# Two chained transformer blocks on one core: logits taken from the unscaled rows, and the gather of the expert tokens as two products of rounded parts

## The reference

```
h = h + mix
u = rmsnorm(h, norm_ffn_w)                      # h / rms(h) * w
g_logits = u @ router_group_w + b               # 4 groups
e_logits = (u @ router_expert_w + b)[group]     # 8 experts in a group
top 2 experts of the best group, weights g_prob * softmax(top 2)
y[token] = sum of weight * (silu(u @ gate[e]) * (u @ up[e])) @ down[e]
out = rmsnorm(h + y, norm_final_w)
```

## Time and profile before

| | |
|---|---|
| median, lowest, highest of 3 runs | 1380.79, 1374.78, 1382.4 us |
| the profiled execution's own time | 1377.91 us |
| its span, first to last instruction | 1376.1 us |
| busy share PE, DVE, ACT, POOL | 94%, 44%, 34%, 4% |
| mean granted clock of PE | 0.978 |
| DMA traffic | 349.86 MB |

### The profile page before, as it was taken

One profiled execution on the slowest core, in us unless ns is written; L12 is line 12 of the kernel. 1 busy time (PEld: TensorE's weight loads), 2 busy tenths in 40 slices (PEclk: granted clock), 3 DMA queues, 4 the chain that ended last, 5 costly groups with the idle time before them and its releaser, 6 DMA issues. The chain is left out here.

```text
span 1376.1 us, 18603 instructions
## 1 busy us (share of the span) xinstructions
PE 1290.4 (94%) x8067; PEld 958.5 (70%) x8067; DVE 605.0 (44%) x925; ACT 470.5 (34%) x688; POOL 60.9 (4%) x57
## 2 busy tenths in 40 slices
PE   6898869999999999799999999889999999999996
PEld 3886758999998989679999999644344443434432
DVE  2776667344556586485755556431110111101112
ACT  3643545433444644444554454211000000000001
POOL 2021000000000121010020000000000000000000
PEclk9999979999999999899999999999999999999999
DMA  9776313675544434344355545859999999999993
GB/s 353 268 264 241 125 59 123 217 243 184 184 138 153 157 125 161 107 157 150 123 161 185 184 162 179 356 242 401 422 421 421 421 420 421 421 421 421 421 421 136
DMA packets 102163, 349.86 MB, mean 254 GB/s; under 512 B 5856, under 2 KB 9216, under 8 KB 77504
## 3 DMA queue, kind: packets, MB, share of 16 engines
q1 hardware_dynamic: 100624, 345.56, 66.4%
q0 software_dynamic: 1168, 2.99, 0.7%
q10 hardware_dynamic: 288, 0.10, 0.0%
HBM read 347.57 MB, written 1.05 MB: 253 GB/s over the span
## 5 line engine op out<-in xcount | busy, mean ns | idle before, releaser
L520 PE MATMUL bank<-XH,WHL 128*128 128x256 f32 x2928 | 544.2, 286 | 16.2 <-DVE WHL L1253 8.6
L520 PEld LDWEIGHTS bank<-XH,WHL 128*128 128x128 f32 x2928 | 464.6, 194 | 22.9 <-issue 10.7
L520 PE MATMUL bank<-XL,WHL 128*128 128x256 f32 x1464 | 416.5, 285 | 0.0
L1253 DVE TENSOR_TENSOR WHL<-weights,WHL 128x1024 fp32r<-128x1024 f32 x223 | 279.7, 1270 | 209.6 <-ACT WHL L872 209.1
L872 ACT ACTIVATE WHL<-weights 128x1024 fp32r<-128x1024 f32 x223 | 231.8, 1054 | 210.4 <-PE bank L520 210.2
L520 PEld LDWEIGHTS bank<-XL,WHL 128*128 128x128 f32 x1464 | 283.9, 194 | 0.2
L520 PE MATMUL bank<-WHL,XH 128*128 128x512 f32 x320 | 106.0, 406 | 9.4 <-DVE WHL L1253 9.4
L1921 DVE TENSOR_TENSOR chainm<-bank,chainm 128x512 f32<-128x512 f32 x16 | 11.1, 692 | 171.9 <-PE bank L818 171.9
L818 PE MATMUL bank<-weights,arena 128*64 128x512 f32 x384 | 84.5, 592 | 0.0
L818 PE MATMUL bank<-arena 128*64 128x512 f32 x384 | 84.4, 592 | 0.0
L520 PEld LDWEIGHTS bank<-WHL,XH 128*128 128x128 f32 x320 | 62.4, 195 | 26.2 <-DVE WHL L1253 11.7
(11 more groups left out here) (313 smaller groups left out, 1137.6 us busy)
## 6 DMA issues: line engine op xcount, KB each, us to landing
...
```

Of the source, the lines that this page charges most:

```text
L520: ins = e.matmul(o, l, r, start=first, skip_group_check=True, stop=g.part == g.parts - 1 and k == g.kc - 1 and n == 2)
L1253: e.tensor_tensor(lo, unit_weights(g, u), hi, ALU.subtract).then_inc(S.w_lo, 1)
```

## The change

`utok` goes away. In its place stand `uhi`, h/rms rounded to fp32r (written by ACT), and `ulo`, the rest (computed by POOL from `full`, h/rms unrounded, which POOL computes too). The norm's weight w no longer goes into the rows: the router's weights are multiplied by it once (POOL), and the gathered columns get it when they leave PSUM (`w8`, ACT and DVE).

The logits are taken from h itself and scaled by 1/rms after the product (L1827 of the changed kernel, in place of the L1805 of before). So PE turns h, one half of the features in the middle of `wf1` and the other behind it, with the roles in the logit product swapped: tokens come out on partitions, and nothing has to be turned back.

`choose` multiplies `uhi` and `ulo` with `pick`, which is fp32r as well (its entries are 0 and 1). `uhi`, `ulo` and `pick` lie in the memory that the split's buffers leave, so `late_weights` has 2 slots in place of 4 and the arena 8 in place of 6. The ring stays at 16.

The overflow count's last part moves from pair 0 to pair 1. The last norm moves into the engines' own streams, token half by token half: `combine` of the last pair goes half by half, ACT squares each quarter, DVE scales it, and SP stores it in four parts of 256 KB, ahead of the flag.

```
-        wrow = b5.take([P, D])
+        w8 = b5.take([P, KC])
...
-        utok = b5.take([P, TT, D])
+        full = Region(2048).take([P, TT, D])
...
                 w.wait_ge(S.m_slots, picked(g))
-                w.wait_ge(S.rn_v, 8)
+                w.wait_ge(S.rn, TT)
+                w.wait_ge(S.rl, TT)
                 for q in range(4):
                     b = 4 + q % 2
                     clear(b)
                     for kk in range(2):
                         k = 2 * q + kk
-                        for j in range(TT):
-                            ins = e.matmul(bank[b][:, kk * T:(kk + 1) * T], utok[:, j, k * P:(k + 1) * P],
-                                           pick[:, j, :], start=j == 0, stop=j == TT - 1)
+                        for i in range(2 * TT):
+                            u, j = (uhi, ulo)[i // TT], i % TT
+                            ins = e.matmul(bank[b][:, kk * T:(kk + 1) * T], u[:, j, k * P:(k + 1) * P],
+                                           pick[:, j, :], start=i == 0, stop=i == 2 * TT - 1)
                     ins.then_inc(S.m_ch, 1)
-                    free[b] = (S.m_xv if q % 2 else S.m_xa, 2 * g + q // 2 + 1)
+                    free[b] = (S.m_xv if q % 2 else S.m_xa, 4 * g + q // 2 * 2 + 2)
 
             def combine(p):
                 w.wait_ge(S.m_wc, p + 1)
-                for n in range(2):
+                for i in range(4):
+                    n, j = divmod(i, 2) if p < NPAIR - 1 else (i % 2, i // 2)
                     w.wait_ge(S.m_ya if n else S.m_yv, p + 1)
-                    for j in range(TT):
-                        b = 2 * j + n
-                        if p == 0:
-                            clear(b)
-                        e.matmul(bank[b][:, :], wpT[p % 2][:, j * P:(j + 1) * P], yo[p % 2][:, n * 512:(n + 1) * 512],
-                                 start=p == 0, stop=p == NPAIR - 1, skip_group_check=True).then_inc(S.m_cb, 1)
+                    b = 2 * j + n
+                    if p == 0:
...
+            def turn_half(c):
+                for j in range(TT):
+                    clear(4 + j)
+                    w.wait_ge(*by[f"wf{c}"].freed[j])
+                    for k in range(4):
+                        ins = e.transpose(bank[4 + j][:, k * P:(k + 1) * P],
+                                          xtok2[:, j, (4 * c + k) * P:(4 * c + k + 1) * P], ident[:, :])
+                    ins.then_inc(S.uT, 1)
+                    free[4 + j] = (S.uTv if c else S.uTa, j + 1)
+                    yield
+
+            def logits(c):
+                for j in range(TT):
+                    if c == 0:
+                        clear(6 + j)
+                        w.wait_ge(S.rw, 1)
+                    w.wait_ge(S.uTv if c else S.uTa, j + 1)
+                    for k in range(4 * c, 4 * c + 4):
+                        ins = e.matmul(bank[6 + j][:, 0:36], uTe[:, k, j * P:(j + 1) * P], rw[:, k, :], start=k == 0,
+                                       stop=k == KC - 1, skip_group_check=True)
+                    if c:
+                        ins.then_inc(S.lg, 1)
+                        free[6 + j] = (S.rt, RT_LG)
+
+            wf1 = gemm("wf1", lambda: logits(0))
+            next(wf1)
+            run(turn_half(0))
+            run(wf1)
+            run(turn_half(1))
+            logits(1)
...
-                if p == 0:
+                if p == 1:
                     clear(6)
                     w.wait_ge(S.ov_v, 3)
                     e.matmul(bank[6][:, 0:2], ones[:, :], over[:, 0:2], start=True, stop=True).then_inc(S.ov_p, 1)
...
-                    e.activation(xg[:, 2 * q:2 * q + 2, :], bank[4][:, :].rearrange("p (k s) -> p k s", k=2),
-                                 ACT.Copy).then_inc(S.m_xa, 1)
+                    for kk in range(2):
+                        k = 2 * q + kk
+                        e.activation(xg[:, k, :], bank[4][:, kk * T:(kk + 1) * T], ACT.Copy,
+                                     scale=w8[:, k:k + 1]).then_inc(S.m_xa, 1)
...
+            def first_features():
+                for j in range(TT):
+                    w.wait_ge(S.uT, j + 1)
+                    e.activation(uTe[:, 0:4, j * P:(j + 1) * P], bank[4 + j][:, :].rearrange("p (k t) -> p k t", k=4),
+                                 ACT.Copy).then_inc(S.uTa, 1)
+            run(gemm("wf1", evac_res(1), before=first_features))
+            w.wait_ge(S.rn_v, 1)
+            e.activation(ss[:, 4:6], ss[:, 4:6], ACT.Sqrt, bias=epsc[:, 0:1], scale=1.0 / D).then_inc(S.rn_a, 1)
+            w.wait_ge(S.rn_v, 2)
             for j in range(TT):
-                sj = ss[:, 4 + j:5 + j]
-                w.wait_ge(S.rn_v, 4 * j + 1)
-                e.activation(sj, sj, ACT.Sqrt, bias=epsc[:, 0:1], scale=1.0 / D).then_inc(S.rn_a, 1)
-                for half in range(2):
-                    i = 2 * j + half
-                    w.wait_ge(S.uT, i + 1)
-                    e.activation(uTe[:, 4 * half:4 * half + 4, j * P:(j + 1) * P],
-                                 bank[4 + i][:, :].rearrange("p (k t) -> p k t", k=4), ACT.Copy).then_inc(S.uTc, 1)
-            w.wait_ge(S.lg, 1)
-            e.activation(lgT[0:36, :], bank[4][0:36, 0:T], ACT.Copy).then_inc(S.lgc, 1)
+                e.activation(by_chunk(uhi)[:, j, :, :], xtok2[:, j, :].rearrange("p (q k) -> p q k", k=KC), ACT.Copy,
+                             scale=ss[:, 4 + j:5 + j]).then_inc(S.rn, 1)
...
-                sj = ss[:, 4 + j:5 + j]
-                w.wait_ge(S.ssq, j + 3)
-                norm(e.tensor_tensor(sj, ss[:, 2 * j:2 * j + 1], ss[:, 2 * j + 1:2 * j + 2], ALU.add))
-                w.wait_ge(S.rn_a, j + 1)
-                norm(e.reciprocal(sj, sj))
-                w.wait_ge(S.rn_v, 4 * j + 2)
-                w.wait_ge(S.d_late, LATE)
-                for half in range(2):
-                    c = slice(half * 512, (half + 1) * 512)
-                    norm(e.scalar_tensor_tensor(out=by_chunk[:, j, 64 * half:64 * half + 64, :],
-                                                in0=xtok2[:, j, c].rearrange("p (q k) -> p q k", k=KC), scalar=sj,
-                                                in1=wrow[:, c].rearrange("p (q k) -> p q k", k=KC), op0=ALU.mult,
-                                                op1=ALU.mult))
+                w.wait_ge(S.uT, TT + j + 1)
+                e.tensor_copy(uTe[:, 4:8, j * P:(j + 1) * P],
+                              bank[4 + j][:, :].rearrange("p (k t) -> p k t", k=4)).then_inc(S.uTv, 1)
+            w.wait_ge(S.ssq, 2 * TT)
+            e.tensor_tensor(ss[:, 4:6], ss[:, 0:4:2], ss[:, 1:4:2], ALU.add).then_inc(S.rn_v, 1)
+            w.wait_ge(S.rn_a, 1)
+            e.reciprocal(ss[:, 4:6], ss[:, 4:6]).then_inc(S.rn_v, 1)
+            w.wait_ge(S.rn_v, 2)
...
-            then(e.tensor_tensor(lg, bank[5][:, 0:72].rearrange("p (j e) -> p j e", j=TT),
-                                 rb.unsqueeze(1).broadcast_to([P, TT, 36]), ALU.add))
+            for j in range(TT):
+                w.wait_ge(S.lg, j + 1)
+                then(e.scalar_tensor_tensor(out=lg[:, j, :], in0=bank[6 + j][:, 0:36], scalar=ss[:, 4 + j:5 + j], in1=rb,
+                                            op0=ALU.mult, op1=ALU.add))
...
+            def added(j, n):
+                o = xtok2[:, j, n * 512:(n + 1) * 512]
+                w.wait_ge(S.m_cb, 4 * (NPAIR - 1) + 2 * j + n + 1)
+                e.tensor_tensor(o, bank[2 * j + n][:, :], o, ALU.add).then_inc(S.acc, 1)
+
+            def summed(j):
+                w.wait_ge(S.t_sq, 2 * j + 2)
+                e.tensor_tensor(small[:, 34 + j:35 + j], small[:, 44 + 2 * j:45 + 2 * j], small[:, 45 + 2 * j:46 + 2 * j],
+                                ALU.add).then_inc(S.t_sum, 1)
+
+            def scaled(j):
+                sj = small[:, 34 + j:35 + j]
+                w.wait_ge(S.t_rms, j + 1)
+                e.reciprocal(sj, sj).then_inc(S.t_rstd, 1)
+                w.wait_ge(S.t_rstd, j + 1)
+                for n in range(2):
+                    c = slice(n * 512, (n + 1) * 512)
+                    e.scalar_tensor_tensor(out=normed[:, j, c], in0=xtok2[:, j, c], scalar=sj, in1=frow[:, c],
+                                           op0=ALU.mult, op1=ALU.mult).then_inc(S.t_out, 1)
+            added(0, 0)
+            added(0, 1)
+            added(1, 0)
+            summed(0)
+            added(1, 1)
+            scaled(0)
+            summed(1)
+            scaled(1)
...
+            w.wait_ge(S.d_late, LATE)
+            w.wait_ge(S.pcol, 1)
+            e.tensor_tensor(rw, rw, pcol[:, ROWS["ffnn"]:ROWS["ffnn"] + KC].unsqueeze(2).broadcast_to([P, KC, 36]),
+                            ALU.mult).then_inc(S.rw, 1)
+
+            w.wait_ge(S.rn_v, 2)
+            for j in range(TT):
+                e.tensor_tensor(by_chunk(full)[:, j, :, :], xtok2[:, j, :].rearrange("p (q k) -> p q k", k=KC),
+                                ss[:, 4 + j:5 + j].unsqueeze(2).broadcast_to([P, P, KC]), ALU.mult).then_inc(S.rf, 1)
```

(17 more changed lines are left out.)

163 lines of the change are left out of this document (81 added, 82 removed).

## The result

The changed kernel takes 1367.24 us (median of 7 runs, 1364.93 to 1369.97), the kernel before 1379.76 (7 runs). The ratio is 0.991, with a 95% interval of 0.9895 to 0.9924. The profiled execution of the changed kernel took 1364.93 us, its span is 1363.0; it is compared with the span of before, 1376.1. The difference is 13.1 us, and three differences between points of the two timelines hold all of it.

What follows compares the result with a forecast made beforehand. PE and the loads were close limits, the loads slower by 2.05 us per two pairs and setting the end. 1377.91 less 8.1 (end of down) less 3.1 (the end) gave 1366.7, said as 1367; own range 1362 to 1371.

Steps and rivals of the forecast that it cites:

- POOL and DVE exclude each other: In the routing, instructions with two SBUF inputs lock each other out whole; DVE advances little until POOL's four end at 890.2.
- The rival without exclusion: POOL and DVE don't exclude each other with instructions this small: first gate product at 893.5, 1357.7 us in all; chance 0.14.
- The size of the routing: From `wf1` to the experts: gather begins at 898.7, 1.4 us later than before; first gate product at 902.6, 1.9 earlier.
- The turns: Turning h on PE: eight turns make `wf1` end 1.8 us later; the second half's turns behind it take 2.2 us.
- POOL's products: Two of POOL's four routing instructions, writing in steps of 512 bytes: 3.0 us each, bounded by 2.4 and 5.6.
- The two products: The gather as 32 fp32r records takes 3.84 us in place of 7.13; rival that they aren't cheaper: 1376, chance 0.07.
- The loads as the bound: Expert stage: cheaper gathers make PE lose its lead from about pair 8, then wait; 17 of 23 us saved become waits.
- the rival of the falling clock: Expert stage from pair 8: PE's clock falls in the waits for loads; 1405 us with 18 slow halves; chance 0.07.
- The end goes by the last landing: Last load lands at 1349.3, half of down (3.6 us) remains: down ends at 1352.9 against 1360.95, 8.1 us less.
- the gap at 958: Load queue partly empty from 958 to 962, some 1.1 us; the earlier refill was to close it.
- PE's clock in the routing: PE idles some 6 us between its spins before the gather, so its clock may fall; nothing counted, 2 us as bound.
- The end: Behind down: last scaling 3.7 us after the last addition, was 6.9; flag beside the stores; gain 3.1, bounds 1 and 4.5.

## Why the prediction was right, and where it was not

**POOL and DVE exclude each other: right.** Four small instructions were held to the end of POOL's, and without POOL's work the gate came 6.6 us earlier. The Trainium skill's rule (SBUF — State Buffer, SBUF: two separate sides) names exactly these pairs, a DVE instruction with two SBUF inputs against one of GpSimd that reads SBUF. The rows here show that it holds for DVE instructions of 8 elements too, and not for those with one input or one in PSUM. The rival without exclusion forecast 1357.7, and it falls.

**The size of the routing: off by 5.8 us.** The first gate product was forecast at 902.6 and came at 896.75. The gather began at 892.49, and by the prediction's own sign ("I am wrong if the gather starts before 893") this part was wrong. Two terms of the sum were too large.
- The turns. I read "1.09 for 8 records" as one group of four turns. It is two groups: a turn is one record. The eight turns in `wf1` cost 1.03 us and not 2.2, and the ones behind `wf1` likewise. 1/rms was there at 875.2 and not at 878.6: 3.4 us, some 2.5 of them the turns. The rest is mostly the logits' first half and the norm's three steps, which were each a little shorter than their price.
- POOL's products: 1.92 us each, not 3.0. With a write in steps of 512 bytes they took less than a difference with a contiguous one, 2.32. They also read a broadcast operand, and no product with a contiguous output was run, so the price of the steps alone is not shown. The Trainium skill (SBUF — State Buffer, Specifications) states a penalty for such an access; with DVE's factor it would have given 3.9, and the trace is against it. Another 2.2 us.

The small terms nearly cancel: 0.8 us for DVE's instructions between POOL's cost POOL nothing, and the stretch behind POOL and the gather were 0.4 us longer each.

**The two products: right.** The first gather took 4.3 us (3.84 forecast) against 7.1.

**The loads as the bound: right.** From the copy at 1132.88 on each pair takes longer than PE's own pace, at 421 GB/s of traffic, and 18.0 us of PE's time turn into waits (17 forecast). The clock stays up: the rival of the falling clock has nothing in the rows.

**"The end goes by the last landing": wrong.** This is the step that failed. The refill began 7.7 us earlier and the last packets came some 10 earlier (the gap at 958 explains 1.1 of the difference, the rest is open). By the rule down would end at 1342.5 + 3.6 = 1346.1; it ended at 1349.1. I took down's second half for the last waiter because its loads are the last. But the loads of up land 9 us before them, and behind up PE has 15.7 us of its own. Moving 3.6 of these brought the end of down 2.2 us forward in the traces.

**PE's clock in the routing: within its bound.** PE idled 7.25 us ahead of L809, at 887.0, and the granted clock was 0.50 to 0.52 from 886 to 892. The 12 spins took 4.85 us, where they take 2.92 at the 2.4 GHz level, but DVE's last selection matrix was ready only at 892.4, as they ended. So they cost nothing, and the gather ran at full clock.

**The end: 1.3 of 3.1 us.** The addition to the last scaling went as worked out (3.6 against 3.7). What failed is "leaving the block and the flag run beside the stores". I had named it as the bound of 1 us; the kernel without the flag's read shows that this read costs 2.9.

The errors have opposite signs: the gate was forecast 5.8 us too late, what follows it 2.1 and 1.8 us too short. For the profiled execution the sum said 1366.7, and it took 1364.93. That the total fits better than its parts is their cancelling, and so luck. The 1367 has a second piece of it: the sum was made against an execution 2.9 us under the median then on record. Taken off that median, its 11.2 us would have given 1369.6; the two medians came out 12.5 apart.
